# State-space groups: the decays' running sums spread by a transfer instead of by TensorE

## What is computed

```python
def ssd_chunked(xh, dt, A, Bm, Cm):
    ...
    a_cs = jnp.cumsum(a, axis=-1)            # running sums of the decays, inside a chunk
    L = segsum_exp(a)                        # exp(cs[l] - cs[s]) for s <= l, else 0
    CB = jnp.einsum('bclgn,bcsgn->bcgls', Cc, Bc)
    y_diag = jnp.einsum('bcgls,bcgrls,bcsgrp->bclgrp', CB, L, x)
    ...
    y_off = jnp.einsum('bclgn,bcgrpn,bcgrl->bclgrp', Cc, prev, jnp.exp(a_cs))
    return (y_diag + y_off).reshape(Bsz, S, H, P)
```

## Time and profile before

| | us |
|---|---|
| median of 3 runs | 2260.74 |
| lowest and highest run | 2259.51, 2265.66 |
| span of the profiled execution, first to last instruction | 2257.3 |
| PE busy in the span | 2160.0 (96%) |
| DVE busy | 1194.3 (53%) |
| ACT busy | 718.8 (32%) |
| POOL busy | 714.8 (32%) |

### The profile page before, as it was taken

One profiled execution on the slowest core, in us unless ns is written; L12 is line 12 of the kernel. 1 busy time (PEld: TensorE's weight loads), 2 busy tenths in 40 slices (PEclk: granted clock), 3 DMA queues, 4 the chain that ended last, 5 costly groups with the idle time before them and its releaser, 6 DMA issues.

```text
span 2257.3 us, 31701 instructions
## 1 busy us (share of the span) xinstructions
PE 2160.0 (96%) x11908; PEld 1561.9 (69%) x11909; DVE 1194.3 (53%) x1881; ACT 718.8 (32%) x1121; POOL 714.8 (32%) x444
## 2 busy tenths in 40 slices
PE   6999999999999999999999999999999989999995
PEld 5877567788878766877777778876555555555553
DVE  6566754899871447788999563245422212222122
ACT  4335754333341333344344345223111111111112
POOL 4331123343354324333333326541122222222220
PEclk9999999999999999999999999999999999999998
DMA  4220132446433223222222213321778899999884
GB/s 162 82 87 1 66 109 78 149 163 210 166 136 119 75 59 110 76 75 75 59 73 75 75 56 112 113 98 75 286 232 290 286 327 321 315 333 351 305 286 147
DMA packets 160926, 350.59 MB, mean 155 GB/s; under 512 B 11552, under 2 KB 100640, under 8 KB 142016
## 3 DMA queue, kind: packets, MB, share of 16 engines
q1 hardware_dynamic: 143360, 304.00, 37.8%
q0 software_dynamic: 15232, 39.02, 7.3%
q10 hardware_dynamic: 2240, 6.29, 0.8%
HBM read 332.48 MB, written 33.55 MB: 162 GB/s over the span
## 4 chain that ended last, share of the span: by engine, by line
PE 86%; DMA 6%; DVE 4%; ACT 2%; issue 1%; POOL 0%; SPq 0%; ACTq 0%; POOLq 0%; DVEq 0%
PE bank L887 24%; PE bank L1591 13%; PE bank L1273 12%; PE bank L1612 7%; PE bank L1194 5%; PE bank L1364 3%; DMA arena<-in_we_gate 2%; PE bank L1570 2%; DMA arena<-in_we_down 2%; PE bank L1013 1%; PE bank L1371 1%; DMA arena<-in_w_up 1%; PE bank L878 1%; PE bank L1446 1%; PE bank L1050 1%
## 5 line engine op out<-in xcount | busy, mean ns | idle before, releaser
L1591 PE MATMUL bank<-arena,hn 128*64 128x256 f32 x3072 | 346.3, 384 | 12.7 <-DMA arena<-in_we_gate 12.0
L1591 PEld LDWEIGHTS bank<-arena,hn 128*64 128x64 f32 x3072 | 233.2, 139 | 138.3 <-issue 44.2
L787 POOL TENSOR_TENSOR w_low_flat<-arena,in_high 128x1024 fp32r<-128x1024 f32 (+1 forms) x73 | 185.9, 2568 | 329.9 <-ACT in_high L1918 329.8
L2851 DVE TENSOR_TENSOR inv<-inv,bank 128x128 f32<-128x128 f32 x96 | 23.3, 284 | 329.1 <-PE bank L1591 329.1
L1612 PE MATMUL bank<-arena 128*64 128x512 f32 x768 | 175.4, 598 | 5.2 <-DVE arena L2857 0.5
L765 POOL TENSOR_TENSOR w_low<-arena,w_high 128x2048 fp32r<-128x2048 f32 x22 | 103.4, 4699 | 162.0 <-ACT w_high L1828 162.0
L1273 PE MATMUL bank<-in_x,in_high 128*128 128x512 f32 x384 | 154.7, 403 | 0.0
L2865 DVE SCALAR_TENSOR_TENSOR sq<-bank,arena 128x512 f32<-128x512 f32 x96 | 72.1, 751 | 151.3 <-PE bank L1612 149.5
L1273 PE MATMUL bank<-in_x,w_low_flat 128*128 128x512 f32 x384 | 151.2, 394 | 0.0
L1273 PE MATMUL bank<-x_low,in_high 128*128 128x512 f32 x384 | 150.9, 393 | 0.0
L887 PE MATMUL bank<-x_high,w_high 128*128 128x512 f32 x336 | 133.5, 397 | 1.8 <-POOL w_low L765 1.8
(11 more groups left out here) (491 smaller groups left out, 4887.2 us busy)
## 6 DMA issues: line engine op xcount, KB each, us to landing
arena<-in_we_gate SPq DMA_DIRECT2D x49, 1024.0 KB
arena<-in_we_up SPq DMA_DIRECT2D x49, 1024.0 KB
arena<-in_we_down SPq DMA_DIRECT2D x49, 1024.0 KB
arena<-in_w_in SPq DMA_DIRECT2D x38, 1024.0 KB, 5.4
arena<-in_w_ada SPq DMA_DIRECT2D x12, 2048.0 KB, 8.0
arena<-in_w_up SPq DMA_DIRECT2D x22, 1024.0 KB, 10.7
arena<-in_w_in SPq DMA_DIRECT2D x17, 512.0 KB, 5.2
arena<-in_w_out SPq DMA_DIRECT2D x4, 2048.0 KB, 9.9
```

The costliest lines, as they stand in the source:

```text
L787: pool_eng.tensor_tensor(in2_tile(j, "low"), in2_tile(j, "whole"), in2_tile(j, "high").bitcast(f32), ALU.subtract).then_inc(S("w_low"), 1)
L1591: ins = nc.tensor.matmul(rows_of(banks[2 + part][:, 0:FE], c), columns_of(moe["xT"][:, p, :], k, c), moe["gu"][:, 2 * p + c, at:at + FE], ...
```

## The change

The running sums go to a small tensor in HBM once (`cum_rows`, 4 chunks by 32 heads by 128 tokens, 64 KB), on ACT's queue, during the pooling branch. For each chunk a transfer on ACT's queue reads the 2 KB row of its four heads and writes it to all 128 partitions of the chunk's `L` buffer (256 KB written). The transfer for chunk n+1 is issued while chunk n is in work, after the copy of its transposes; the first two are issued ahead of the groups. `Ex` and L0 read `L` in SBUF where they read bank 4 in PSUM; L0 now works in place. The four matmuls of each chunk, the wait before them, the two parts, the selector and the instructions that made them are gone. The sums are no longer split into two rounded parts but are carried as plain float32.

```diff
@@ PE @@
-            pe.wait_ge(S("dtp_sums"), 4)
...
-                    if n >= 1:
-                        pe.wait_ge(S("L0_done"), HPG * n)
-                    for j in range(HPG):
-                        hd = HPG * g + j
-                        ins = nc.tensor.matmul(banks[4][:, j * P:(j + 1) * P],
-                                               CUM_PICK[2 * SH:4 * SH, hd:hd + 1].to_broadcast([2 * SH, P]),
-                                               cum_parts[2 * SH:4 * SH, now], start=True, stop=True)
-                    ins.then_inc(S("cum_ready"), 1)
@@ ACT, pooling branch, i == 4 @@
+                    act.dma_start(cum_rows.rearrange("c h n -> h c n"),
+                                  pool["acs"][0:SH, :].rearrange("h (c n) -> h c n", n=P)).then_inc(S("cum_stored"), 16)
...
-            act.wait_ge(S("dtp_sums"), 3)
-            nc.scalar.activation(cum_parts[2 * SH:3 * SH, :], cum_high[0:SH, :].bitcast(f32), ACT.Copy)
@@ ACT, groups @@
+            def load_sums(n):
+                g, c = divmod(n, TT)
+                if n >= 2:
+                    act.wait_ge(S("y_ready"), n - 1)
+                act.dma_start(ssd["L"][:, n % 2, :], cum_rows[c, HPG * g:HPG * g + HPG, :].rearrange("h n -> (h n)")
+                              .unsqueeze(0).to_broadcast([P, HPG * P])).then_inc(S(f"cum_in{n % 2}"), 16)
+            act.wait_ge(S("cum_stored"), 16)
+            load_sums(0)
+            load_sums(1)
...
-                    act.wait_ge(S("cum_ready"), n + 1)
+                    if 1 <= n < SG * TT - 1:
+                        load_sums(n + 1)
+                    act.wait_ge(S(f"cum_in{n % 2}"), 16 * (n // 2 + 1))
...
-                    nc.scalar.activation(ssd["Ex"][:, n % 2, :], banks[4][:, :], ACT.Exp).then_inc(S("Ex_done"), 1)
+                    nc.scalar.activation(ssd["Ex"][:, n % 2, :], ssd["L"][:, n % 2, :], ACT.Exp).then_inc(S("Ex_done"), 1)
@@ DVE, ahead of the groups @@
-            nc.vector.tensor_copy(cum_high[0:SH, :], sums).then_inc(S("dtp_sums"), 1)
-            nc.vector.tensor_tensor(CUM_PICK[2 * SH:4 * SH, :], ident[2 * SH:4 * SH, 2 * SH:3 * SH],
-                                    ident[2 * SH:4 * SH, 3 * SH:4 * SH], ALU.add).then_inc(S("dtp_sums"), 1)
-            dve.wait_ge(S("dtp_sums"), 3)
-            nc.vector.tensor_tensor(cum_parts[3 * SH:4 * SH, :], sums, cum_high[0:SH, :].bitcast(f32), ALU.subtract)\
-              .then_inc(S("dtp_sums"), 1)
@@ DVE, groups @@
-                        nc.vector.tensor_scalar(ssd["L"][:, b, j * P:(j + 1) * P], banks[4][:, j * P:(j + 1) * P],
+                        nc.vector.tensor_scalar(ssd["L"][:, b, j * P:(j + 1) * P], ssd["L"][:, b, j * P:(j + 1) * P],
```

More of the change, by code:

```diff
@@ L214, in two_blocks @@
                    a=(T,), acs=(T,))
-        cum_parts = rounded("cum_parts", [P, T], arena_at + 4 * mix["end"])
-        cum_high = rounded("cum_high", [P, T], arena_at + 4 * (dtk["end"] + 6 * (PAD + T) + 2 * PAD))
-        CUM_PICK = rounded("cum_pick", [P, SH], small_at + 4 * 120)
         ssd = lay(dtk["end"], zs=(4, T), xs=(4, T), B=(2, T), C=(2, T), xtok=(2, 3 * P),
@@ L256, in two_blocks @@
         y_rows = nc.dram_tensor("y_halves", (2 * Y_ROWS, D), f32, kind="Internal").ap()
+        cum_rows = nc.dram_tensor("cum_rows", (TT, SH, P), f32, kind="Internal").ap()
         moe = lay(0, gu=(4, 2 * KD * FE), dn=(4, 2 * D))
```

## The result

| | before | changed |
|---|---|---|
| median, us | 2262.03 (4 runs, 2259.51 to 2265.66) | 2237.98 (4 runs, 2230.68 to 2238.77) |
| ratio to before | | 0.9886, 95% interval 0.9868 to 0.9903 |
| span of the profiled execution | 2257.3 | 2228.8 |
| first y product to last, in the groups | 944.6 to 1289.0: 344.4 | 943.2 to 1263.9: 320.7 |

The kernel got 24.0 us faster, 1.1%. The forecast started from the median of three runs of before, 2260.74; a fourth run has moved it to 2262.03. So the time is 5.2 us under the forecast and the gain 6.5 above it.

A forecast was written before the change was run, and what follows sets the result against it. PE was taken to bound the groups. 17.9 us saved there less 0.4 of waiting in chunk 0, all else nothing, gave 17.5 off 2260.74: 2243.2 us, range 2238 to 2252.

The forecast's parts named there:

- What bounds the kernel: In the eight groups PE waits for nobody, busy 349.00 of 349 us; removed work shortens the program one for one.
- What PE loses: Removing four matmuls saves PE 0.56 us a chunk; times 32 chunks, 17.9 us (14.1 to 18.9).
- changes of kind: PE's surcharge between sorts of matmul: 0.21 us ahead of the four, 0.26 behind; one was to remain.
- The bounds: PE's saving per chunk: 0.44 us if both surcharges stayed, 0.59 if the one remaining step costs 0.21.
- L0: DVE's tensor_scalar, now reading SBUF: 286 ns instead of 342, four in a row taking 0.22 us less.
- Chunk 0: In groups 1 to 7 PE waits here for DVE's `M`, nothing to about 0.1 us; 0.05 x 7 = 0.4 taken.
- ACT: One issue per chunk, 0.34 us, between transposes' copy and `Ex`, covered by idle time; `Ex` at same distance; cost nothing.
- The transfers: Loads issued one chunk ahead have 11.3 us in the example; 256 KB lands in 2.4 and 6.9; price nothing.
- Blocking of L0 by GpSimd: Rival, 4%: GpSimd passes hold two of chunk 0's four L0, 4.1 us, for seven groups 29: 2272 us.
- The late transfer: Rival, 3%: landing above some 11.5 us delays `Ex` in chunks 1 to 3, up to 24 us per microsecond.
- given back in the expert stage: Rival, 8%: expert loads do not start earlier, gain turns into waits for weights; half gives 2252 us, all 2260.

The follow-up runs named there:

- the pair of 64 and 128 rows: Changed kernel with four matmuls put back on PE at the removed ones' place, using 64 rows (2260.41 us) or all 128 rows (2248.76 us).
- load_late: Changed kernel with each transfer issued in its own chunk instead of one chunk ahead; 2255.52 us in a single execution.

## Why the prediction was too low

- **What bounds the kernel.** Right. PE was dense before and after, and the time came out of its list; only in chunk 0 does DVE come last, by 0.08 us.
- **What PE loses.** This is the term that was mis-sized: 0.56 us a chunk instead of 0.78. The prediction split the 0.80 us from the second C by B matmul to the first projection into the spacings of the four and two "changes of kind", 0.21 ahead of them and 0.26 behind, and kept one of the two, since it took it for what the step from a float32 product to the rounded projections costs. That step costs nothing: with the block gone, the first projection starts 0.03 us behind the second C by B matmul, where 0.21 to 0.26 were kept. Both changes of kind belonged to the block of 64-row matmuls, as the pair of 64 and 128 rows shows. The 0.26 was also misread: the first of the four lasts 0.32 us and the others 0.27, so the fourth starts at 1068.02, not 1067.96, and only 0.20 lies behind it. What lies behind the first projection plays no part, 0.33 us before and 0.32 after. The bounds, 0.44 and 0.59, both rested on it that something of the surcharge must remain, and so the range was too narrow on the fast side. 31 x (0.78 - 0.56) is 6.8 us, and the miss of the gain is 24.0 - 17.5 = 6.5. That the time came out only just below the range says little: the unedited repeat lies 4 us under it.
- **L0.** Forecast 286 ns and 0.22 us saved for four; measured 282 at the median and 0.25. The estimate from the Trainium skill (VectorE: DVE Perf Modes, the TRN2 errata table), 127 ns and 0.5 us for four, did not hold; the measurement decides.
- **Chunk 0.** Forecast 0.05 us of waiting in each, measured 0.08, with PE arriving 0.22 us earlier than supposed. With L0 from PSUM it is 0.33.
- **ACT.** The cost was nothing, as forecast. The issue runs beside the copy ahead of it and `Ex` came earlier, not at the same distance.
- **The transfers.** Hidden, 3.3 us to land. That 128 partitions read the same 2 KB, which no row of before showed, did not make it slow: the landing lies between the 2.4 and 6.9 us of other 256 KB transfers.
- **The rivals.** Blocking of L0 by GpSimd is real and costs what was said, but does not occur where L0 stands. The late transfer did not occur. Its price, up to 24 us for each microsecond beyond the slack, looks overstated: in load_late `Ex` waits 2.7 us on average, and that cost 8.0 us in all, 0.33 for each of 24 chunks. A landing of more than 11 us itself was not tried. Nothing was given back in the expert stage.
- **Tail and noise.** The stretch from the last product with the branch weights (1446.2 before, 1421.1 changed) to the end took 811.1 us before, and 807.7 and 808.9 in two profiles of the changed kernel; other kernels with the same code there had 808 to 814. Nothing is read into it.

## What to carry to other kernels

When matmuls are taken out of a dense stream, measure the hole from the last steady spacing in front to the first steady spacing behind, not from start to start of the block: the steps into and out of the block carried 0.41 of the 0.80 us here. Count the whole hole as saved where the instruction removed is the only one of its shape, and set as the fast bound that no surcharge stays. Where a step moves from PSUM to SBUF on VectorE, look in order of time for GpSimd passes over that place; with none there the move cost nothing here, and with one there L0 took as long as the pass.

## What was not expected of the hardware

- A block of matmuls that use 64 of the 128 rows, set into a stream of 128-row matmuls, cost 0.34 us for the block beside 0.11 us for each of 128 columns; the same block with all 128 rows cost 0.11 each and nothing more. At a second place the block's surcharge was 0.30, and behind products of 64 columns about 0.15.
- A transfer's issue on ACT's queue (338 ns) ran beside the activation ahead of it in the list.
- Four tensor_scalar of 128 columns from SBUF lasted as long as the pair of GpSimd passes that they met, 5.17 us against 0.87 alone.
